# One Trainium2 core, a two-block network in split fp32: the output of the gated network's first sixteen tiles by seven products in place of eight, from forms written to DRAM

## Time and profile before

| | us |
|---|---|
| median of 3 runs (3432.41 to 3436.12) | 3436.06 |
| the profiled execution | 3436.31 |
| its span | 3434.5 |
| PE busy | 3366.4 (98%) |
| DVE / ACT / POOL busy | 1686.5 (49%) / 1363.0 (40%) / 1388.7 (40%) |
| gated network's first sixteen pairs, first to last matmul on PE | 1379.17 to 1861.05 |
| second network's output by sevens | 3185 to 3420 |

### The profile page before, as it was taken

One profiled execution on the slowest core, in us unless ns is written; L12 is line 12 of the kernel. 1 busy time (PEld: TensorE's weight loads), 2 busy tenths in 40 slices (PEclk: granted clock), 3 DMA queues, 4 the chain that ended last, 5 costly groups with the idle time before them and its releaser, 6 DMA issues.

```text
span 3434.5 us, 46272 instructions
## 1 busy us (share of the span) xinstructions
PE 3366.4 (98%) x18366; PEld 2715.4 (79%) x18366; DVE 1686.5 (49%) x2296; ACT 1363.0 (40%) x2114; POOL 1388.7 (40%) x875
## 2 busy tenths in 40 slices
PE   7999999999999999999999999999999999999998
PEld 5888887777777878788888878888886887888786
DVE  6333324545534877655554354023355246555587
ACT  5333234344323555433332356233323353344444
POOL 2311123444422564866664654311121565444102
PEclk9999999999999999999999999999999999999999
DMA  4221213231234523111112334212343432344743
GB/s 118 78 62 46 67 59 93 73 107 50 74 125 153 198 86 106 55 55 56 56 53 68 95 104 129 74 60 84 99 139 100 127 92 74 125 151 167 232 125 96
DMA packets 387237, 335.97 MB, mean 98 GB/s; under 512 B 16304, under 2 KB 328496, under 8 KB 385232
## 3 DMA queue, kind: packets, MB, share of 16 engines
q1 hardware_dynamic: 356560, 286.88, 27.2%
q10 hardware_dynamic: 30464, 46.14, 4.0%
HBM read 260.72 MB, written 72.25 MB: 97 GB/s over the span
## 4 chain that ended last, share of the span: by engine, by line
PE 82%; DVE 6%; ACT 3%; POOL 3%; issue 3%; DMA 1%; SPq 0%; POOLq 0%; DVEq 0%; ACTq 0%
PE psum L1974 26%; PE psum L281 14%; PE psum L2604 14%; PE psum L2634 6%; PE psum L1592 5%; PE psum L4529 5%; PE psum L1108 2%; PE psum L587 2%; POOL w_lo L1925 2%; PE psum L1639 1%; PE psum L1189 1%; ACT w_hi L1906 1%; POOL m_lo L2088 0%; PE psum L1629 0%; PE psum L1101 0%
## 5 line engine op out<-in xcount | busy, mean ns | idle before, releaser
L1925 POOL TENSOR_TENSOR w_lo<-w_raw,w_hi 128x1024 fp32r<-128x1024 f32 (+1 forms) x239 | 573.0, 2397 | 1160.6 <-ACT w_hi L1906 1138.9
L1906 ACT ACTIVATE w_hi<-w_raw 128x1024 fp32r<-128x1024 f32 (+1 forms) x243 | 251.3, 1034 | 464.0 <-PE psum L1974 423.7
L281 PE MATMUL psum<-x_hi,w_hi 128*128 128x512 f32 x832 | 360.6, 433 | 7.4 <-ACT gate L325 3.9
L1974 PE MATMUL psum<-x_hi,w_hi 128*128 128x512 f32 x912 | 341.4, 394 | 2.5 <-DVE w_lo L1934 1.0
L1974 PE MATMUL psum<-x_hi,w_lo 128*128 128x512 f32 x912 | 336.9, 389 | 0.0
L1974 PE MATMUL psum<-x_lo,w_hi 128*128 128x512 f32 x912 | 336.8, 389 | 0.0
L281 PE MATMUL psum<-x_hi,w_lo 128*128 128x512 f32 x832 | 327.9, 394 | 0.0
L281 PE MATMUL psum<-x_lo,w_hi 128*128 128x512 f32 x832 | 326.6, 393 | 0.0
L1974 PEld LDWEIGHTS psum<-x_hi,w_hi 128*128 128x128 f32 x912 | 170.8, 188 | 42.6 <-issue 6.3
L281 PEld LDWEIGHTS psum<-x_hi,w_hi 128*128 128x128 f32 x832 | 157.1, 189 | 58.4 <-issue 19.4
L1974 PEld LDWEIGHTS psum<-x_lo,w_hi 128*128 128x128 f32 x912 | 171.2, 188 | 37.0 <-issue 1.9
(11 more groups left out here) (781 smaller groups left out, 7901.0 us busy)
## 6 DMA issues: line engine op xcount, KB each, us to landing
w_raw<-in_w_in SPq DMA_DIRECT2D x105, 512.0 KB, 4.5
merge_raw<-gates ACTq DMA_DIRECT2D x48, 512.0 KB, 4.4
x_raw<-mlp_forms SPq DMA_DIRECT2D x91, 256.0 KB, 3.0
gates<-gate SPq DMA_DIRECT2D x32, 512.0 KB, 3.0
w_raw<-in_w_ffn_up SPq DMA_DIRECT2D x60, 256.0 KB, 3.0
mlp_forms<-mlp_staged SPq DMA_DIRECT2D x13, 1024.0 KB, 3.9
w_raw<-in_w_ffn_up SPq DMA_DIRECT2D x24, 512.0 KB, 3.9
mlp_forms<-x_raw SPq DMA_DIRECT2D x13, 768.0 KB, 6.3
```

The source lines that it names most:

```text
L281: last = pe.matmul(bank, w[:, k, :], x[:, k, half(h)], start=(k == 0 and j == 0), stop=(k == KT - 1 and j == 2))
L1906: act.activation(self.view(self.c.wh, i), self.view(self.c.wr, i), ACT.Copy).then_inc(self.sig["w_hi"], 1)
L1925: pool.tensor_tensor(self.view(self.c.wl, i), self.view(self.c.wr, i), self.view(self.c.wh, i).bitcast(F32), ALU.subtract).then_inc(self.s ...
L1974: last = pe.matmul(self.bank(t, h)[0:m, :], w[:, k, col:col + m], x(k)[:, 512 * h:512 * h + 512], start=(k == 0 and n == 0), stop=(k == nk ...
```

## The change

It does the gated network's output in the scheme and the order of the second network's:

- `Gated` does its sixteen pairs back to back on a ring of all eight banks (`RING`, `product_number`); product n waits for what was read eight products before it. The plain output (`plan_out`, `tensor_out`, `scalar_out`, `pool_out`, `vector_out`) goes. h is no longer split; two pairs of h are the four blocks b11, b12, b21, b22 of `down.staged`, and after each odd pair DVE makes the four differences (`less`): t1, t3, t2 and t4.
- The sums of weights s1 to s4 of pairs 2 to 15 are made by DVE (`feed.elsewhere`, `sums_after` in `vector_in`), and no longer by POOL.
- SP stores the seven forms of each two pairs to DRAM, and fetches them as `Down` does. `Down` runs with 8 pairs: 7 x 8 = 56 steps of 12 matmuls, 672 in place of 768.
- Behind the pairs, in `vector_in` of the last one, DVE makes the differences first and then the low parts of the first six forms.
- The splits of weights in this Down are POOL's, but for products 3 and 4 (`own`), which are DVE's. The four last adds stand behind the last step (`LAST` = 0, here the constructor's argument `end`).
- SP waits for the last event of the feed, which is the end of Down's last step, before the quarter of x and the first two strips of class `Ffn`.
- In both networks Down keeps one block of weights per pair (`rows[j]`), and loads a block for every step: `LOADED` says which. In the second network this makes 39 more loads of 256 KB, one sum in each step of products 3, 4, 5 and 6 in place of two in product 3 and one in products 4 and 6; DVE splits the blocks of products 1 to 6, POOL all thirteen of product 0; and the add of a kept product in product 4 writes to PSUM in place of SBUF.

The core of the diff:

```diff
 class Gated(Sevens):
-    FREES = ("h0", "edge1", "edge1", None, "u2", "u3", "u4")
+    READ = (None, "u2", "u3", "u4", "edge1", "edge1", "h0")
+    RING = (7, 4, 6, 5, 3, 0, 2, 1)
...
-        elif p == 2 and n < 3:
-            self.summed(pe, "h1", 0)
+            return
+        before = self.product_number(p, n) - 8
+        if before >= 0:
+            self.bank_read(pe, 1 + before // 7, before % 7)
...
     def pool_in(self, pool, p):
         for u in self.blocks(p):
-            self.feed.lo(pool, u + Feed.PLACES)
-        for h in range(2):
-            pool.wait_ge(self.sig["h_hi"], 2 * p + h + 1)
-            pool.tensor_tensor(self.half_lo(p, h), self.raw(p, h), self.hh(p)[:, half(h)].bitcast(F32), ALU.subtract
...
+        def less(x, y, out, n):
+            dve.wait_ge(sig["forms"], sig.at("forms", 4 * j + n))
+            dve.tensor_tensor(out, x, y, ALU.subtract).then_inc(sig["forms"], 1)
...
         add(3, u3, self.raw(p, 1))
         add(3, u2, u2)
+        if after and p + 1 in self.feed.elsewhere:
+            self.feed.sums_after(dve, after[0][0])
+        if odd:
+            down.stored(dve, j)
+            self.summed(dve, "h1", p - 1)
+            less(b12, b11, t1, 0)
         add(4, s1, banks[4])
...
         add(6, u3, banks[6])
+        if after and p + 1 in self.feed.elsewhere:
+            self.feed.sums_after(dve, after[4][0])
         gate(0, "c21", banks[6])
         gate(1, "c22", self.raw(p, 1))
+        if odd:
+            self.summed(dve, "h1", p)
+            less(b22, b12, t3, 1)
+            less(b22, t1, t2, 2)
+            less(b21, t2, b12, 3)
+        if p == self.PAIRS - 1:
+            for s in range(6):
+                down.lo(dve, s)
...
+        down = Down(core, sig, feed, "ffn", 0, COUNT, a["w_ffn_down"], [b[:, :, :] for b in staged],
+                    [x_raw[:, 4 + i, half(0)] for i in range(3)], w_homes, h_raws, h_places, (0, 0, gated.PAIRS),
+                    ((4, 6, 5, 3), (0, 2, 1, 7)), 0, (3, 4))
+        feed.elsewhere.update(range(2, gated.PAIRS))
...
-            gated.done(sp, gated.outs[gated.PAIRS - 3][-1][1][-1][2])
+            for p in range(LAST):
+                feed.fetch(sp, 4 * p + 11)
+                if p % 2:
+                    sp.wait_ge(sig["forms"], sig.at("forms", 4 * (p // 2 + 1)))
+                    down.store(sp, p // 2, (p // 2) % 2)
...
+            for s in STEPS:
+                if s >= 6:
+                    down.fetch(sp, s)
+                if s >= 10:
+                    down.fetch_w(sp, s)
+            gated.done(sp, feed.events)
             sp.wait_ge(sig["p"], 16 * 2)
             sp.dma_start(quarter_in[:, :, :], quarter_out).then_inc(sig["p"], 16)
...
+            for s in STEPS:
+                i, j = down.product(s)
+                down.sums(dve, s + down.PLACES)
+                down.splits(dve, s + feed.PLACES, True)
+                down.lo(dve, s + down.PLACES)
+                if i and j < 4:
+                    down.add(dve, i - 1, j)
+            for m in range(4):
+                down.add(dve, 6, m)
...
 class Down
-    SUMMED = (3, 4, 6)
+    LOADED = ((0, 0), (0, 1), (1, 1), (1, 0), (1, 1), (0, 0), (0, 1))
...
+        out, x, y, op = {3: (row, row, slot, ALU.subtract), 4: (row, slot, row, ALU.subtract),
+                         5: (slot, slot, row, ALU.add), 6: (slot, slot, row, ALU.subtract)}[i]
+        dve.tensor_tensor(out, x, y, op).then_inc(sig["w_sum"], 1)
...
+    def splits(self, eng, s, own):
+        if s < len(self.blocks) and (s >= Feed.PLACES and self.product(s)[0] in self.own) == own:
+            self.feed.lo(eng, self.blocks[s])
...
-                dve.tensor_tensor(kept, kept, src, ALU.add).then_inc(self.sig["added"], 1)
+                dve.tensor_tensor(src, src, kept, ALU.add).then_inc(self.sig["added"], 1)
...
-                src = kept
```

More of the change, by code:

```diff
@@ L3658, in _, with early_hi @@
                     halves.last_hi(act)
+            def early_hi(n):
+                for s in {3: (0, 1), 4: (2, 3), 5: (4, 5)}.get(n, ()):
+                    gated.done(act, gated.pairs[LAST][n - 2][1])
+                    down.hi(act, s)
             for p in range(gated.PAIRS):
-                gated.scalar_in(act, p)
-                if p >= 2:
-                    gated.scalar_out(act, p - 2)
-            for p in range(gated.PAIRS - 2, gated.PAIRS):
-                gated.scalar_out(act, p)
+                gated.scalar_in(act, p, early_hi if p == LAST else lambda n: None)
+            for s in STEPS:
+                i, j = down.product(s)
+                feed.hi(act, down.blocks[s] + feed.PLACES)
+                down.hi(act, s + down.PLACES)
+                if i == 1 and j < 4:
+                    down.keep(act, j)
             for i in range(2):
@@ L3819, in _ @@
                 gated.pool_in(pool, p)
-                if p >= 2:
-                    gated.pool_out(pool, p - 2)
-            for p in range(gated.PAIRS - 2, gated.PAIRS):
-                gated.pool_out(pool, p)
+            for s in STEPS:
+                down.splits(pool, s + feed.PLACES, False)
             for i in range(2):
@@ L4434, in plan @@
                 self.tile_ends[i, m] = self.steps[N * i + N - 1]
+        if not self.LAST:
+            self.tile_ends.update({(6, m): self.steps[-1] for m in range(4)})
+            return
         for m in range(4):
@@ L4447, in bank @@
     def bank(self, i, m):
-        return self.c.ps[:, m if i % 2 else 4 + m, :]
+        return self.c.ps[:, self.banks[i % 2][m], :]
     def posts(self, i, m):
@@ L4490, in fetch_w @@
     def fetch_w(self, sp, s):
-        if s < len(self.loads) and self.loads[s] is not None:
+        if s < len(self.loads):
             self.feed.fetch(sp, self.loads[s])
```

211 lines of the change are left out of this document (95 added, 116 removed).

## The result

The changed kernel took 3442.09 us (median of 10 runs, 3438.33 to 3446.40), the kernel before 3433.63 us in ten runs of its own (3430.48 to 3436.69): the ratio is 1.0024, with a 95% interval of 1.0015 to 1.0034, so about 8.5 us slower. The three runs shown before the prediction lay 2.4 us above that ten-run median. I had forecast 3438.7 us, 2.6 us slower than before; the time lies in my range, the shift is three times what I said, and the median has just passed the 0.2% that I took for "the same" (the interval reaches down to 0.15%).

The account below looks back on a forecast made before the run. PE, busy 98% of the span, was taken as the bound, so time is matmul count plus PE's waits. Terms -21.76 - 1.2 + 8.8 + 12.5 + 4.35 = +2.7 us gave 3438.7 us, range 3430 to 3450 (8 in 10).

Parts of the forecast that it names:

- Removed: 96 matmuls: Gated network's output: 672 matmuls in place of 768, all on PE's path, -21.76 us.
- Start of the stage: First matmuls of the gated network: two bank waits for ACT go, 0.3 us taken back, -1.2 us.
- Steady state: Sixteen pairs: DVE needs 35.1 to 36.2 us for two pairs against PE's 38.08, so cost 0.
- first rival: In the pairs, DVE fails to keep up through collisions with POOL over sums and differences: 3448 us, chance 0.25.
- Hand-over to the output stage: After the last pair, PE waits 7.1 us for DVE's differences and first split, plus 1.7 slow clock: +8.8 us.
- Output stage: The 56 steps of the gated network's Down: DVE and transfers keep up with PE, 0 us.
- Hand-over to class Ffn: After Down's last step, quarter, strips and splits leave PE idle 10.8 us, plus 1.7 slow clock: +12.5 us.
- Tail: End of the second network's Down: seven added sums in product 5 lengthen DVE's chain, +4.35 us (2 to 6).
- The 0.9 for a slow clock: Part of the second network's end: a longer PE wait brings the low clock about every second time, 0.9 us.
- the 0.33 for slower: Whole kernel: chance 0.33 given to a slower result, against 0.55 for the same and 0.12 for faster.
- The rival of cheaper hand-overs: Both stage changes and the second network's end cost less: 3432 us, or 3430 without collisions there; chance 0.22.

Follow-up runs that it names:

- Forms first: Changed kernel with SP issuing the first six fetches of forms before the loads of weight blocks 4 and 5; ratio 1.0016 to the kernel before.
- three low parts first: Changed kernel with forms fetched before weight blocks 4 and 5, and DVE splitting forms 0 to 2 before add 6 of the last pair; ratio 0.9994.
- the mended kernels: Changed kernel with queue orders, places and waits at both hand-overs reworked, sums on POOL: 3413.46 us; with second network's old Down 3411.69, with sums on DVE instead 3416.79.
- the strips early: Changed kernel with SP's wait before class Ffn narrowed, so the first two strips and the quarter of x load sooner; ratio 1.0006 to the kernel before.

## Why the prediction was right or wrong, step by step

- **Removed: 96 matmuls, -21.76.** Right; they are gone from the page's count and A follows the pitch.
- **Start of the stage, -1.2.** The two bank waits (1.5) went and nothing replaced them, the 0.8 stayed: -1.5.
- **Steady state, 0, "35.1 to 36.2 us for two pairs".** PE has no wait, as forecast, but for another reason than mine, and so it was in part luck. DVE takes 38.26, because I added up its own operations and left out what it would wait for: three times 2.0 us for a split by POOL. So it had none of my 2 to 3 us to spare, and kept the lag of 5 to 6 us with which it enters the pairs (5.2 in pair 3, 6.1 in pair 15). The ring of eight banks hid it while the pairs lasted, and it came out at the hand-over. My first rival had this place and asked for three more collisions; it was waits, not collisions.
- **Hand-over to the output stage, +8.8 (7.1 and 1.7).** This is the step that failed. It measured 14.2 us and 2.4 for the clock (A's 485.8 less 457.0, 0.8, 14.2 and 10.4 leave 3.4 us for the slow clock and the joints), some 8 us more than my term. I followed DVE alone from the end of product 6, as if it stood where it stands in pair 10. Two queues were left out: SP's, where the fetches of forms stand behind loads that wait for POOL, and ACT's, where the forms' high parts stand ahead of the tap that DVE needs. Forms first took 5.0 us off, three low parts first 5.0 more.
- **Output stage, 0.** Right: no wait of PE in its 56 steps, though DVE's low parts took 1.36 us beside POOL's splits in products 0 to 2. (The 287 GB/s that I called the busiest row is the mean of 35 us; the earlier trace rows has 385 in 2 us. Nothing hung on it.)
- **Hand-over to class Ffn, +12.5 (10.8 and 1.7).** The wait was 10.44 (the steps that I listed add up to 10.7, not 10.8), and the pitch then 0.427 for eight matmuls, 1.6 us. From it to Down of the second network the stretch is only 0.2 us longer than before, since there the slow clock of before at 2035 (below) did not come, by chance: four of the fourteen profiles have it.
- **Tail, +4.35.** The cause is right (253.4 and 253.5 us without the sums), size and path are not: it costs some 2.4 us. I let seven sums lengthen a chain of DVE that PE would meet at its end. PE's waits at that end did not change (0.3 and 0.2 us); the sums reach PE earlier, over ACT's order and POOL's squares, as one wait of 1.75 at L4654. The 0.9 for a slow clock, "about every second time", rests on no run: after the 1.75 the granted clock stays at 1.00. That one profile showed 4.2 was chance.
- **The forecast** of "the same" came from a sum that was some 8 us short at the first hand-over and 2 too long at the tail; by the median the 0.33 for slower was the better bet, by a margin within the noise. The rival of cheaper hand-overs was wrong as the change stands, and is what the mended kernels became.

## What to carry to other kernels

Where a deep ring of buffers hides how late an engine is, "no wait" in the steady state is no proof that the engine keeps up: compare its period with that of the bound, and look how far it lies behind. An engine without spare time keeps the lag with which it starts, and that is paid where the ring ends. At every change of stage follow each in-order queue separately, that of SP and that of ACT too: a fetch behind a load that waits, and a copy of data that has not landed ahead of one that others need, cost 5.0 us here, and a high part that waits for a sum, ahead of a square, cost PE 1.75 us in the other network. And a small operation moved from DVE to POOL is not free for DVE when both read from SBUF.

## What the hardware showed that I had not expected

- After the wait of 14.2 us the pitch was 0.427 for twelve matmuls (granted clock 0.50, the 1.2 GHz level), where the waits of 2.4 and 8.2 us before the change had eight; at 1700.63 it was back. I had taken 1.7 us for it, and 2.4 is right here (twelve times 0.2). The longer wait is not the reason: in four other profiles a wait of 14.8 to 15.1 us was followed by eight or nine such matmuls, in "forms first" one of 9.2 by fourteen, and with the strips early the 2.7 us that open the second network's Down by none.

```profile
1696.00:1700.00 4.00, 4.00 (x11) 3.14 (x10) 2.28 (x4) 0.00 (x0) 0.00 (x0) 0.50 0.98 346
1701.00:1705.00 4.00, 4.00 (x20) 3.27 (x19) 0.88 (x2) 2.29 (x4) 2.00 (x2) 1.00 0.65 181
```

- Two waits of 0.9 us within 2 us let the clock fall in one execution and not in another, with the same instructions: in the profile of before the window from 2035 has clock 0.67, in that of the changed kernel, with the same two waits, 1.00. That is 1.6 us of difference between two executions, for nothing that the kernels do. The windows of before, then of after:

```profile
2035.00:2040.00 5.00, 5.00 (x17) 3.94 (x16) 3.84 (x6) 0.00 (x0) 2.46 (x2) 0.67 0.54 158
```

```profile
2035.00:2040.00 5.00, 4.30 (x19) 3.60 (x20) 4.48 (x7) 0.94 (x2) 3.70 (x3) 1.00 0.60 176
```
